# Rounding the weights on GpSimd, cutting the normed x straight from its bank, and product groups inside the last stick-breaking pair

## What is computed

```python
def hybrid_layer(x, ...):                      # twice: first block
    h = rms_norm(x, norm_mix)
    proj = h @ w_in                            # split into the inputs of four mixers and the gates
    ys = [nsa_mixer(...), stick_breaking_mixer(...), gla_mixer(...), forgetting_mixer(...)]
    branch = einsum('bsnc,ncd->bsnd', ys, w_branch)
    mixed = sum(sigmoid(gate_logits + b_gate) * branch, axis=2)
    x = x + mixed @ w_out
    h2 = rms_norm(x, norm_ff)
    return x + square(relu(h2 @ w_ff1)) @ w_ff2

def second_block(x, ctx, c, ...):              # layer 0: GQA over x and 256 context tokens; layer 1: MLA
    for i in range(2):
        h = x * (1 + scale(c)) + shift(c)
        x = layer_norm(alpha * x + gate(c) * mixer_i(h, ...))
        x = layer_norm(alpha * x + gate(c) * (square(relu(h' @ w1)) @ w2))
    return x
```

## Time and profile before

| | us |
|---|---|
| median of 3 runs | 2491.93 |
| lowest and highest | 2489.9, 2492.78 |
| the profiled execution | 2486.95 |
| its span, first to last instruction | 2485.1 |
| TensorE busy in the span | 2275.7 |
| VectorE busy | 1167.8 |
| ScalarE busy | 1124.8 |
| POOL busy | 16.3 |
| mean granted clock of TensorE, share of full speed | 0.958 |

### The profile page before, as it was taken

The page is one execution under the profiler, slowest core; times in us unless marked ns, Lnnn a source line. Parts: engine busy times, 40 slices in busy tenths (PEclk is TensorE's granted clock), DMA queues, the critical chain, the costliest instruction groups (busy, mean ns, idle before and its releaser), DMA issues. The chain is left out here.

```text
span 2485.1 us, 33805 instructions
## 1 busy us (share of the span) xinstructions
PE 2275.7 (92%) x14023; PEld 1839.9 (74%) x14023; DVE 1167.8 (47%) x1618; ACT 1124.8 (45%) x1758; POOL 16.3 (1%) x23
## 2 busy tenths in 40 slices
PE   5999999989969999999899798898999998997998
PEld 4898777979858987778798554445788886454987
DVE  3464443755424553436554304655334434375565
ACT  3444656366323436654564236733243231363543
POOL 0000000000000000000000000000000000100000
PEclk9998999989979999998899898998999999998999
DMA  7532566545355326565445222003122213212451
GB/s 201 205 136 103 204 237 219 171 170 197 143 140 190 136 70 236 208 225 191 173 171 203 111 106 73 1 1 117 70 102 102 95 51 89 96 40 85 170 181 73
DMA packets 209912, 341.24 MB, mean 137 GB/s; under 512 B 46435, under 2 KB 77598, under 8 KB 209630
## 3 DMA queue, kind: packets, MB, share of 16 engines
q1 hardware_dynamic: 207068, 334.68, 38.6%
q0 software_dynamic: 944, 3.47, 0.5%
q10 hardware_dynamic: 1746, 0.89, 0.1%
HBM read 335.88 MB, written 3.15 MB: 136 GB/s over the span
## 5 line engine op out<-in xcount | busy, mean ns | idle before, releaser
L261 PE MATMUL bank<-hT_high,ring_low 128*128 128x256 f32 (+1 forms) x2032 | 606.6, 299 | 0.0
L261 PEld LDWEIGHTS bank<-hT_high,ring_low 128*128 128x128 f32 x2032 | 390.6, 192 | 12.4 <-issue 0.5
L248 DVE TENSOR_TENSOR ring_low<-ring,ring_high 128x2048 fp32r<-128x2048 f32 (+2 forms) x108 | 239.8, 2220 | 222.3 <-ACT ring_high L241 221.9
L260 PE MATMUL bank<-hT_low,ring_high 128*128 128x256 f32 (+1 forms) x1008 | 296.5, 294 | 15.7 <-ACT work L1005 7.5
L262 PE MATMUL bank<-hT_high,ring_high 128*128 128x256 f32 (+1 forms) x1008 | 288.5, 286 | 0.0
L241 ACT ACTIVATE ring_high<-ring 128x2048 fp32r<-128x2048 f32 (+2 forms) x108 | 200.3, 1855 | 156.6 <-PE bank L262 127.3
L260 PE MATMUL bank<-ring_low,hidden_high 128*128 128x512 f32 x640 | 254.0, 397 | 0.0
L1005 ACT ACTIVATE work<-bank 128x512 f32<-128x512 f32 (+8 forms) x264 | 120.0, 481 | 217.2 <-PE bank L262 170.1
L260 PEld LDWEIGHTS bank<-hT_low,ring_high 128*128 128x128 f32 (+1 forms) x1008 | 193.7, 192 | 27.2 <-issue 16.0
L248 DVE TENSOR_TENSOR ring_low<-ring,half_high 128x2048 fp32r<-128x2048 f32 x64 | 146.4, 2292 | 136.8 <-ACT half_high L241 136.8
L262 PEld LDWEIGHTS bank<-hT_high,ring_high 128*128 128x128 f32 (+1 forms) x1008 | 193.5, 192 | 0.4
(11 more groups left out here) (228 smaller groups left out, 4396.2 us busy)
## 6 DMA issues: line engine op xcount, KB each, us to landing
ring<-w_ff SPq DMA_DIRECT2D x32, 2048.0 KB, 8.2
ring<-mlp_w SPq DMA_DIRECT2D x32, 2048.0 KB, 8.2
ring<-w_in SPq DMA_DIRECT2D x30, 2048.0 KB, 7.8
ring<-w_ada SPq DMA_DIRECT2D x24, 2048.0 KB, 8.0
ring<-w_branch SPq DMA_DIRECT2D x24, 512.0 KB, 6.4
ring<-w_in SPq DMA_DIRECT2D x32, 256.0 KB, 4.1
ring<-w_out SPq DMA_DIRECT2D x4, 2048.0 KB, 7.6
ring<-gqa_w_qkv SPq DMA_DIRECT2D x3, 2048.0 KB, 16.1
```

The costliest lines, as they stand in the source:

```text
L248: nc.vector.tensor_tensor(self.part(i, True), self.part(i, False), self.high(i).bitcast(F32), ALU.subtract)\
L260: nc.tensor.matmul(out, a[0], b[1], start=start, stop=False)
L261: nc.tensor.matmul(out, a[1], b[0], start=False, stop=False)
```

## The change

Three edits; VectorE's cuts of the weights keep their places.

1. All roundings of weights leave ScalarE. `make_high` becomes `round_high`, a `tensor_copy` on GpSimd, in a POOL program of its own for the first block and between POOL's other work in the second. POOL takes the parts in their order of use, each as soon as its tile has landed and its buffer is free. Two parts of the feed-forward wait for the last branch product, the rest of it for the last out product; in the second block the first three of a layer wait for the last attention output.
2. `take_hT` makes only the rounded form, eight copies in place of sixteen. `low_bits` computes scaled bank minus rounded form directly from the bank, in two instructions of 256 columns per chunk in place of one of 512 from SBUF, and now frees the bank. TensorE waits for the banks to be free instead of for `hT_cut`.
3. The first two of the sixteen branch groups (`branch_part(0, 0)` and `branch_part(0, 1)`, the gated linear attention and nsa) move from behind the pair loop into its last step, ahead of `turned(15)` and of `output(15)`.

```diff
@@ -231,14 +231,12 @@
         _, k, n = self.part(i, True).shape
         return self.buffers[i % len(self.buffers)][:, 0:k * n].rearrange("p (k n) -> p k n", k=k)
 
-    def make_high(self, nc, act, *which):
-
-        for i in which:
-            if i < len(self.parts):
-                self.weights.arrived(act, self.parts[i][0])
-                if i >= len(self.buffers):
-                    act.wait_ge(*self.freed[i - len(self.buffers)])
-                nc.scalar.activation(self.high(i), self.part(i, False), ACT.Copy).then_inc(self.high_made, 1)
+    def round_high(self, nc, pool, i):
+
+        self.weights.arrived(pool, self.parts[i][0])
+        if i >= len(self.buffers):
+            pool.wait_ge(*self.freed[i - len(self.buffers)])
+        nc.gpsimd.tensor_copy(self.high(i), self.part(i, False)).then_inc(self.high_made, 1)
 
     def make_low(self, nc, dve, *which):
...
@@ -653,7 +651,7 @@
             turn_x("xT", TT)
 
 
-            pe.wait_ge(hT_cut, KD // 2)
+            PROJ.taken(pe, "xT2", "xT3")
             for i in range(2):
                 pair(f"q{i}", f"q{i}", 0)
             for i, name in enumerate(("kc", "vc")):
@@ -920,13 +918,32 @@
                     thin(PROJ.claim(pe, f"ada{n}"), silu_c, w, KD).then_inc(PROJ.full, 1)
 
 
+            def branch_part(f, at):
+
+                n = BRANCHES[at]
+                if f == 0:
+                    pe.wait_ge(y_cut, max(count for group, count in y_count.items() if group[0] == n))
+                y = [y_high[n], [y_low[:, 4 * n + c, :] for c in range(4)]]
+                w = Y.arrived(pe, f"branch{f}", 8 * (at // 2))
+                ps = PROJ.claim(pe, f"br{n}_{f}")
+                for k in range(2):
+                    for c in range(4):
+                        last = product(nc, ps[:, k * S:(k + 1) * S], [part[:, 4 * (at % 2) + c, k * P:k * P + P] for part in w],
+                                       [part[c] for part in y], c == 0, c == 3)
+                last.then_inc(PROJ.full, 1)
+
+
             PROJ.taken(pe, "vs", "vwg")
             SC.taken(pe, "vc2")
             for m in range(PAIRS + 1):
                 if m < PAIRS:
                     filler(2 * m)
+                else:
+                    branch_part(0, 0)
                 if m >= 1:
                     turned(m - 1)
+                if m == PAIRS:
+                    branch_part(0, 1)
                 later = m >= 1 and jobs[2 * m - 2][0] == "sb"
                 if later and m < PAIRS:
                     filler(2 * m + 1)
@@ -941,17 +958,9 @@
 
 
             for f in range(KD // 2):
-                for at, n in enumerate(BRANCHES):
-                    if f == 0:
-                        pe.wait_ge(y_cut, max(at for group, at in y_count.items() if group[0] == n))
-                    y = [y_high[n], [y_low[:, 4 * n + c, :] for c in range(4)]]
-                    w = Y.arrived(pe, f"branch{f}", 8 * (at // 2))
-                    ps = PROJ.claim(pe, f"br{n}_{f}")
-                    for k in range(2):
-                        for c in range(4):
-                            last = product(nc, ps[:, k * S:(k + 1) * S], [part[:, 4 * (at % 2) + c, k * P:k * P + P] for part in w],
-                                           [part[c] for part in y], c == 0, c == 3)
-                    last.then_inc(PROJ.full, 1)
+                for at in range(4):
+                    if f > 0 or at > 1:
+                        branch_part(f, at)
             for h in range(2):
                 banks = [PROJ.claim(pe, f"wo{h}{t}") for t in range(TT)]
                 for b in range(2):
...
@@ -1025,10 +1033,8 @@
                 for c in range(4):
                     ps = PROJ.arrived(act, f"{name}{c}")
                     for k in range(2):
-                        copy(high[:, 2 * c + k, :], ps[:, k * S:k * S + S], scale=cols[:, row + 2 * c + k:row + 2 * c + k + 1])
-                    copy(hT[:, 2 * c, :], ps[:, 0:S], scale=cols[:, row + 2 * c:row + 2 * c + 1])
-                    copy(hT[:, 2 * c + 1, :], ps[:, S:2 * S], scale=cols[:, row + 2 * c + 1:row + 2 * c + 2])\
-                        .then_inc(PROJ.free(f"{name}{c}"), 1)
+                        copy(high[:, 2 * c + k, :], ps[:, k * S:k * S + S], scale=cols[:, row + 2 * c + k:row + 2 * c + k + 1])\
+                            .then_inc(hT_rounded, 1)
...
@@ -1244,8 +1228,17 @@
-                X.make_high(nc, act, i + 4)
-            X.make_high(nc, act, *range(FFK // 2 + 4, FFK))
+
+        @block.gpsimd
+        def _(pool):
+            for i in range(len(parts)):
+                Y.round_high(nc, pool, i)
+            pool.wait_ge(*done(f"br{BRANCHES[-1]}_{KD // 2 - 1}"))
+            for i in range(2):
+                X.round_high(nc, pool, i)
+            pool.wait_ge(*done("wo11"))
+            for i in range(2, len(halves)):
+                X.round_high(nc, pool, i)
...
-            def low_bits(high):
-
+            def low_bits(name, row, high):
+
+                base = KD * (high is hT_high[1])
                 for c in range(KD // 2):
-                    part = slice(2 * c, 2 * c + 2)
-                    PROJ.taken(dve, f"{'xT' if high is hT_high[0] else 'yT'}{c}")
-                    vec.tensor_tensor(hT_low[:, part, :], hT[:, part, :], high[:, part, :].bitcast(F32), ALU.subtract)\
-                        .then_inc(hT_cut, 1)
+                    ps = PROJ.arrived(dve, f"{name}{c}")
+                    dve.wait_ge(hT_rounded, base + 2 * c + 2)
+                    for k in range(2):
+                        last = vec.scalar_tensor_tensor(hT_low[:, 2 * c + k, :], ps[:, k * S:k * S + S],
+                                                        cols[:, row + 2 * c + k:row + 2 * c + k + 1],
+                                                        high[:, 2 * c + k, :].bitcast(F32), ALU.mult, ALU.subtract)
+                    last.then_inc(PROJ.free(f"{name}{c}"), 1)
...
+            highs(0, 0, 3)
             norm_rows(0, 1, ln_count[0, 0, NT[0] - 1])
+            highs(0, 3, own)
             norm_rows(1, 0, ln_count[0, 1, NT[0] - 1])
```

47 lines of the change are left out of this document (11 added, 36 removed).

## The result

The changed kernel takes 2473.23 us (median of five runs, 2471.83 to 2475.21) where the kernel before, with two more executions beside its three, took 2491.93 (2484.84 to 2492.78): a ratio of 0.993, 95% interval 0.9917 to 0.9942, so 14.5 to 20.7 us faster. The forecast for the median was 2470, the range 2452 to 2502. Measured once more, beside the kernel before, it took 2473.47 us, ratio 0.9932 (0.9918 to 0.9945).

The account below looks back on a forecast made before the run. TensorE, busy 2275.7 of 2485.1 us, was taken as the bound, so only its idle places could gain. Terms summed to -11.0 us per layer, twice -22: 2465 profiled, 2470 with 5.0 added for the median; range 2452 to 2502.

Parts of the forecast that it names:

- Start of a layer: First products of a layer: 0.5 us later, since VectorE's first weight cut stands ahead of freeing the banks.
- Second norm: Norm at the layer's end: products 1.3 us earlier by a shorter chain; collisions there priced separately at 3.1.
- the sum of all collisions: POOL roundings blocking VectorE at the norm, branch products and levels: 7.6 us per layer together, the middle, +3.8, taken.
- Behind the compressed keys: TensorE's 1.79 us wait at 117.13 for a ScalarE copy held by a rounding goes: -1.8 us per layer.
- Decay levels: VectorE's loop from 140 to 206 us loses its 0.99 us waits for roundings: 3 of 4.0 us per layer returned.
- Before the gates: TensorE's waits for ScalarE at 237.62 and 250.38: all 0.90 and 1.0 of 1.59 go, -1.9 us per layer.
- Last stick-breaking pair: The 1.68 us wait goes and two branch groups cover 3.95 more, with 0.8 left: -4.8 us per layer.
- Clock: Granted clock partly returns where the 1.79 and 3.28 us waits vanish: between nothing and 5, half taken, -2.5 per layer.
- No collisions: Rival: POOL roundings do not hold up VectorE, collision term zero; -14.8 us per layer, 2462 us; chance 0.18.
- Full exclusion: Rival: VectorE stands for what is left of each rounding, term 7.6; -7.2 us per layer, 2478 us; chance 0.20.
- Waits only move: Rival: levels' loop still delays TensorE, banks come free no earlier; within 5 us of 2491.9; chance 0.10.
- Slow rounding: Rival: POOL's rounding takes well over 1.85 us; 2504 us at 3.8, 2543 at 4.5; chance 0.16.

Follow-up runs that it names:

- start_low_first: Changed kernel, but VectorE takes the normed x's low part ahead of its first weight cut at each first-block layer's start; 2467.47 us, ratio 0.9913.
- keys_later: Changed kernel, but GpSimd rounds part 11 only once the compressed keys' hidden values are done and their bank is free; 2471.21 us, ratio 0.9916.
- the cover: Kernel before with only two branch products moved under the last stick-breaking pair, roundings still on ScalarE; 2486.86 us, ratio 0.9997.

## Why the forecast was right, and where it was not

**The total.** 2470 against 2473.2, inside the narrower 2463 to 2476 too. But the profiled execution was to take 2465 and took 2473.4. The sum was 8.4 us too generous; the median came out near by luck, because the step from the profiled execution to the median was wrong the other way. It added 5.0 us to the profiled time of after, as they stood between median and profile of before. That distance was the spread of the kernel before with its clock. In the kernel after, median and profiled execution are 0.2 us apart. The same step is missing in the lower end of the range: 2452 is 2 x 17.3 below the profiled 2486.95; for the median it is 2457.

**The rounding itself**: 1.95 us against 1.9. The nearest row, a plain copy with a quarter of the partitions, was the right one.

**Start of a layer, +0.5**: measured +0.65 and +0.5, for the reason given; start_low_first shows that this reason was worth an edit of its own.

**Second norm, -1.3 and 3.1 for the collision**: the shorter chain gave 1.1, the collision cost 2.6. Mechanism and size right; the lengthened cut and scalings are the two places it named. Halving the sum of all collisions was no good guess for this term: here the upper end held.

**Behind the compressed keys, -1.8**: failed. The wait of the earlier trace rows is gone, as said, but a wait 14 us earlier grew by as much, from 1.61 to 3.40 us. Clock, TensorE's busy time and the rest in two windows, first before:

```profile
100.00:108.00 8.00, 6.39 (x54) 6.05 (x53) 3.63 (x6) 2.43 (x3) 0.00 (x0) 1.00 0.65 250
112.00:120.00 8.00, 6.21 (x42) 5.60 (x41) 3.76 (x7) 6.08 (x10) 0.00 (x0) 0.79 0.62 217
```

then after:

```profile
100.00:108.00 8.00, 4.61 (x27) 4.50 (x26) 4.69 (x6) 0.63 (x3) 1.89 (x1) 0.79 0.59 228
112.00:120.00 8.00, 8.00 (x69) 7.45 (x68) 3.57 (x2) 4.07 (x9) 2.91 (x2) 1.00 0.26 71
```

Half of the low clock moved with the wait: 3.4 us at half clock behind the new wait, 6.8 behind the old one. The other half came back where no wait is near. TensorE from 130 to 142 us, first in the kernel after, then in the second execution of the same kernel that was profiled (changed_again):

```profile
130.00:142.00 12.00, 12.00 (x98) 11.61 (x96) 7.96 (x8) 5.16 (x8) 3.11 (x2) 0.86 0.50 176
```

```profile
130.00:142.00 12.00, 12.00 (x111) 11.47 (x110) 8.21 (x8) 4.34 (x7) 3.32 (x2) 1.00 0.51 176
```

TensorE is busy in all 12 us of both, and in the kernel after it had been so, at full clock, for the 26.9 us from 108.0 to 134.9; then the clock was at half for 3.4 us, which cost 1.5. In changed_again the wait of 3.40 us is the same, this drop is missing, and the place gains 1.3 us in layer 1, all of it clock.

The step looked for collisions in three places, chosen by how busy VectorE was and how large its operations were; the one that cost most after the norm was an operation of 0.19 us in a chain that TensorE waits for. That is the step that failed, and keys_later shows it. With 2.14 us left there (1.61 before) the wait itself would still be half a microsecond longer than before; why, was not tried.

**Decay levels, -3.0**: -3.3 in both layers, collisions included, against -2.5. That is near by luck. Of the waits only 1.7 us per layer came back (on the masked copies 7.9 us in all became 4.5), not 3 less 0.5; the other 1.6 is a stretch of 3.4 us at half clock, at 198.5 us in layer 1, that is gone. The term for the waits was too large and one for the clock was missing here.

**Before the gates, -1.9**: -0.9 and -0.5. The first wait is gone as said. The second, of which 1.0 was to go, grew:

```profile
244.24 0.55 PE L258 MATMUL bank<-hT_low,ring_high 128*128 128x256 f32 x1 [2.91 <-ACT work L1013]
```

TensorE came there 7.5 us earlier, ScalarE's squares and table loads only 6.1: 1.3 of what TensorE had gained it waited off again. What the place gained in layer 1 is all clock. The term took a wait as removed where its chain, not the rounding, was late.

**Last stick-breaking pair, -4.8, and branches, +1.75**: -4.5 and -7.9, against -3.1. The waits: 0.24 and 1.01 left where 0.8 was forecast, so that the sign "none over 0.5 at the last pair" did not hold, and 0.8 from blocked additions, under the 1.75 for the branch stage. By idle time it is -3.5 and -3.6, as forecast within half a microsecond. What was missed is the clock behind the 3.28 us, 1.0 us in layer 1 and 4.3 in layer 2, which stood in the clock's term as a part of 2.5 for the whole layer.

**Clock, -2.5 per layer, 5**: 6.9 in all. Its size was near, a middle taken between bounds; its cause was not an account of single waits: the feed-forward lost 0.9 in each layer.

**Feed-forward and second block, 0**: +0.9 per layer and +1.5. In the second block roundings block VectorE too (twelve additions by 0.9 to 1.1 us each, four cuts by 1.7), and TensorE's waits there did not grow with them; the 1.5 appear at other places, with the clock, and stay unexplained.

**The rivals.** No collisions: refuted. Full exclusion, 2478 for the median: its mechanism is shown, its time was 5 us too high for the median. On the profiled execution it gives 2472.6 against 2473.4, but by terms that cancel: the branch stage hides what it was charged for, the compressed keys and the gates cost what it did not have. Waits only move: true of two places of six. Slow rounding: refuted by the row of 1.95.

## What to carry to other kernels

Before moving elementwise work to GpSimd, list the VectorE instructions without a bank operand that can begin while it runs, and price them by the chain that they stand in, not by their length: an operation of 0.19 us that TensorE waits for, held up for 1.1, cost more than 8 us in a stage with slack. Where parts of a change are tried one by one, a part that brings nothing alone may be the one that the others need: the cover showed no gain alone, and 11.8 us beside the rest. When an engine is relieved, read what stands first in the order of the engine that is next late: one line moved in VectorE's gave 4 us by the ratios, 6 by the medians. Before a forecast starts from a profiled execution, see where that execution lies among the others: here it lay 5 us under the median, and that step hid an error of 8.
